# Gate and up projections as seven block products per feature tile instead of eight, and the dense stage in four parts of tiles

## The reference

```python
D_MODEL = 1024
D_FF = 2816

def swiglu(u, w_gate, w_up, w_down):
    return (jax.nn.silu(u @ w_gate) * (u @ w_up)) @ w_down

h = rms_norm(x, g_pre2) * (1 + scale2) + shift2
x = x + gate2 * rms_norm(ffn(h), g_post2)
```

## Time and profile before

| | before |
|---|---|
| median of 3 runs | 2035.15 us |
| the profiled execution, own time | 2034.17 us |
| its span | 2032.4 us |
| granted TensorE clock, mean | 0.976 |
| busy: PE, DVE, ACT, POOL | 1911.1 (94%), 1300.1 (64%), 1084.6 (53%), 96.8 us (5%) |
| gate and up matmuls of the dense stage (L2832) | 2112, first at 472.7, last at 893.9 us |
| down matmuls, parts 1 and 2 (L2864); last part (L2886) | 480, to 809.4 us; 180, to 937.7 us |

### The profile page before, as it was taken

How to read it: one execution, slowest core, us unless ns; L and a number is a source line. 1 busy time by engine, 2 the same in 40 slices (tenths; PEclk the granted TensorE clock), 3 DMA queues, 4 the chain that set the end, 5 groups by cost and what they waited for, 6 DMA issues and landing times. The chain is left out here.

```text
span 2032.4 us, 31748 instructions
## 1 busy us (share of the span) xinstructions
PE 1911.1 (94%) x11144; PEld 1613.2 (79%) x11144; DVE 1300.1 (64%) x1977; ACT 1084.6 (53%) x1781; POOL 96.8 (5%) x64
## 2 busy tenths in 40 slices
PE   5998899899999999998998899889999999999998
PEld 2995575599998998997995665887888888888885
DVE  3735666575223233346817766657888888888888
ACT  4225654454211211236226654547888888888885
POOL 0330000000000000000410000002000000000002
PEclk9998899899999999998999999899999999999999
DMA  6203622202222213212216701149978191918394
GB/s 261 98 27 144 227 85 90 101 18 73 78 83 89 78 52 99 75 61 68 98 47 237 272 23 43 63 154 383 410 283 329 53 360 44 359 63 319 113 320 188
DMA packets 132849, 303.41 MB, mean 149 GB/s; under 512 B 20496, under 2 KB 66448, under 8 KB 129680
## 3 DMA queue, kind: packets, MB, share of 16 engines
q1 hardware_dynamic: 126608, 279.51, 37.9%
q10 hardware_dynamic: 3264, 12.07, 1.5%
q0 software_dynamic: 2880, 10.49, 1.3%
HBM read 360.43 MB, written 28.10 MB: 191 GB/s over the span
## 5 line engine op out<-in xcount | busy, mean ns | idle before, releaser
L2587 DVE TENSOR_TENSOR ex_wl<-ex_raw,ex_wh 128x1024 fp32r<-128x1024 f32 x351 | 419.6, 1223 | 25.8 <-ACT ex_wh L2426 13.8
L2426 ACT ACTIVATE ex_wh<-ex_raw 128x1024 fp32r<-128x1024 f32 x351 | 367.6, 1060 | 70.8 <-PE psum L2506 44.6
L2832 PE MATMUL psum<-norm_out,ex_w_hi 128*128 128x320 f32 x1408 | 268.9, 309 | 2.9 <-PEq L1771 2.9
L2506 PE MATMUL psum<-ex_wh,ex_he_hi 128*128 128x512 f32 (+1 forms) x624 | 242.3, 388 | 4.2 <-DVE ex_wl L2587 3.2
L2506 PE MATMUL psum<-ex_wl,ex_he_hi 128*128 128x512 f32 (+1 forms) x624 | 233.1, 374 | 0.0
L2506 PE MATMUL psum<-ex_wh,ex_he_lo 128*128 128x512 f32 (+1 forms) x624 | 232.6, 373 | 0.0
L2832 PEld LDWEIGHTS psum<-norm_out,ex_w_hi 128*128 128x128 f32 x1408 | 223.1, 188 | 3.2 <-DVE ex_w_lo L2693 3.1
L2693 DVE TENSOR_TENSOR ex_w_lo<-side,ex_w_hi 128x1024 fp32r<-128x1024 f32 (+1 forms) x82 | 82.7, 1015 | 165.4 <-ACT ex_w_hi L2689 165.1
L2832 PE MATMUL psum<-norm_out,ex_w_lo 128*128 128x320 f32 x704 | 165.8, 308 | 0.0
L2767 ACT ACTIVATE ex_sg_hf<-psum 128x640 f32<-128x640 f32 x22 | 15.5, 706 | 235.3 <-PE psum L2832 235.3
L2506 PEld LDWEIGHTS psum<-ex_wh,ex_he_hi 128*128 128x128 f32 x624 | 118.0, 189 | 26.8 <-issue 5.4
(11 more groups left out here) (462 smaller groups left out, 3901.1 us busy)
## 6 DMA issues: line engine op xcount, KB each, us to landing
ex_raw<-moe_gate_up SPq DMA_DIRECT2D x221, 512.0 KB
ex_raw<-moe_w_down SPq DMA_DIRECT2D x143, 512.0 KB
x<-moe_gate_up SPq DMA_DIRECT2D x64, 512.0 KB
wmod_ssd<-w_mod SPq DMA_DIRECT2D x56, 512.0 KB, 5.8
wmod_at<-w_mod SPq DMA_DIRECT2D x24, 512.0 KB, 4.1
side<-ffn_w_gate SPq DMA_DIRECT2D x22, 512.0 KB, 3.9
side<-ffn_w_up SPq DMA_DIRECT2D x22, 512.0 KB, 3.9
mx_qkv_room<-w_in SPq DMA_DIRECT2D x10, 1024.0 KB, 4.9
```

Source lines behind the costliest of these rows:

```text
L2426: act.activation(wh[:, i % RING], raw_of(i), ACT.Copy).then_inc(*hi_done.up(1))
L2506: last = pe.matmul(p.psum[:, 2 + g % 2, 0:width], h[:, k], w[:, i % RING, cols], start=(k == 0 and m == 0), stop=(k == KD - 1 and m == 2))
L2587: dve.tensor_tensor(wl[:, i % RING], raw_of(i), wh[:, i % RING].bitcast(F32), ALU.subtract).then_inc(*lo_done.up(1))
L2832: last = pe.matmul(p.psum[:, home[i] + half, 0:HT], m[:, i % w.RING, cols], x[:, k, half * HT:(half + 1) * HT], start=(k == 0 and n == 0), ...
```

## The change

From the fourth feature tile on, gate and up of a tile are computed together as one product of 2x2 blocks. The tokens are cut in two halves (first, second; 320 each) and the channels in two (top, bottom; 4 blocks of 128 each), which gives token blocks a11, a12 (first half; top, bottom), a21, a22 (second half). The weights have the blocks gate top, gate bottom, up top, up bottom, each 128 x 512 floats. Instead of eight block products there are seven of 12 matmuls each, on combinations:

- tokens: s1 = a21 + a22, s2 = s1 - a11, s4 = a12 - s2, s3 = a11 - a21; made once, on GpSimd (s1, s2, s4: seven additions of 128 x 1280 floats) and VectorE (s3: three), then split in high (ScalarE) and low (VectorE);
- weights, per tile, on VectorE, in the raw room, four subtractions of 512 columns: t1 = up top - gate top, t2 = up bottom - t1, t3 = up bottom - up top, t4 = gate bottom - t2;
- the seven products (`PRODUCTS`) are gate top by a11, t1 by s1, t2 by s2, gate bottom by a12, t3 by s3, up bottom by s4, t4 by a22. t2, t3 and t4 are added in the bank of gate top, up bottom in the bank of t1, and between them the intermediate sums are copied out (ScalarE: `keep_p1`, `keep_p5`, `keep_u2`, 320 columns each) and mixed (VectorE: `mix_gate`, `mix_second`, `mix_first`).

The pieces become entries of 512 columns in rings of 8, made six entries ahead (`ahead_by`). There are four raw rooms. The high part of the hidden tile moves from VectorE to ScalarE (`hidden_high`). The parts are (6, 6, 6, 4). The gate rows are loaded only after the last feature tile, since their room is s1's.

```diff
-DENSE_PARTS = (8, 8, 6)
+DENSE_PARTS = (6, 6, 6, 4)
+PLAIN_F = 3
+PRODUCTS = ("gate_top", "t1", "t2", "gate_bottom", "t3", "up_bottom", "t4")
...
-    RING = 6
+    RING = 8
+    RAW = 4
...
+        @block.gpsimd
+        def _(pool):
+            link = chained(pool_c)
+            pool.wait_ge(*before.low.at(1))
...
+            link(pool, pool.tensor_tensor(s1, plain(a21[0]), plain(a22[0]), ALU.add))
+            link(pool, pool.tensor_tensor(s1, s1, plain(a21[1]), ALU.add))
+            pool.tensor_tensor(s1, s1, plain(a22[1]), ALU.add).then_inc(*token_sum.up())
...
         @block.scalar
...
+            for e in range(n_plain, whole[0]):
+                kind, f, n = entries[e]
+                if kind == "t1":
+                    keep_p1(f)
+                if kind == "t2":
+                    keep_p5(f)
+                if kind == "gate_bottom":
+                    keep_u2(f)
+                if e and entries[e - 1][0] == "t4":
+                    silu_second(entries[e - 1][1])
+                make(e + ahead_by)
+                if kind == "t3":
+                    silu_first(f)
+                if e and entries[e - 1][0] == "t4":
+                    hidden_high(entries[e - 1][1])
...
+            hidden_high(n_f - 1)
+            act.wait_ge(*rows_out.at(16))
+            act.dma_start(rows[:], p.gate_rows.rearrange("q c -> (q c)").partition_broadcast(P)).then_inc(*rows_in.up(16))
...
         @block.tensor
+                if kind == "t1" and f == PLAIN_F:
+                    pe.wait_ge(*token_low.at(3))
+                if kind == "t2":
+                    pe.wait_ge(*copied.at(3 * g + 1))
+                if kind == "t3":
+                    pe.wait_ge(*copied.at(3 * g + 3))
...
+                if kind == "up_bottom":
+                    pe.wait_ge(*copied.at(3 * g + 2))
+                if kind == "t4":
+                    pe.wait_ge(*mixed.at(3 * g + 2))
+                product(e, kind in ("gate_top", "t1", "gate_bottom"))
...
         @block.vector
+            def make(e):
...
+                dve.wait_ge(w.hi_done, e + 1)
+                w.block_low(dve, e)
+                if kind == "gate_top":
+                    dve.wait_ge(*w.arrival(entry_of("up_bottom", f)))
+                    dve.wait_ge(w.lo_done, e + 1)
+                    combine(f, "t1")
...
+            for e in range(n_plain, whole[0]):
+                if kind == "t3":
+                    mix_gate(f)
+                if kind == "up_bottom":
+                    mix_second(f)
+                if kind == "t4":
+                    mix_first(f)
+                make(e + ahead_by)
+                if before_kind == "t4":
+                    multiply(before_f)
+                if e >= 2 and entries[e - 2][0] == "t4":
+                    hidden_low(entries[e - 2][1])
```

More of the change, by code:

```diff
@@ L2835, in features, with product @@
                 return last
+            def product(e, fresh):
+                name, f, _ = entries[e]
+                x_hi, x_lo = moving[name]
+                for k in range(HALF_K):
+                    cols = slice(k * P, (k + 1) * P)
+                    for n, (m, x) in enumerate(((w.wh, x_hi), (w.wh, x_lo), (w.wl, x_hi))):
+                        last = pe.matmul(bank(name, f), m[:, e % w.RING, cols], x[:, k],
+                                         start=(fresh and k == 0 and n == 0), stop=(k == HALF_K - 1 and n == 2),
+                                         skip_group_check=not fresh)
+                last.then_inc(*used.up())
             for i in range(front):
-                pe.wait_ge(w.lo_done, i + 1)
+                pe.wait_ge(w.lo_done, 2 * i + 2)
                 if i == 2:
@@ L2859, in _ @@
                     for b in range(TB):
[L2860 removed]
+                        out = units[part_of[f], n][b]
                         if f == first_of[f]:
[L2862 to L2865 removed]
+                            claim([out])
@@ L2866, in _ @@
+                        for m, (y, x) in enumerate(((hh, w.wh), (hh, w.wl), (hl, w.wh))):
+                            last = pe.matmul(p.psum[:, out, :], y[:, tile, b * P:(b + 1) * P], x[:, e % w.RING, 0:512],
+                                             start=(f == first_of[f] and m == 0), stop=(f == last_of[f] and m == 2))
                         if f == last_of[f]:
                             sums += 1
-                            held[bank] = (evicted, sums)
-                else:
-                    claim([home[i], home[i] + 1])
-                    last = features(i, range(2))
-                    held[home[i]] = held[home[i] + 1] = (taken, f + 1)
@@ L2945, in _ @@
             before.keep_low(dve, TB - 1)
[L2946 to L2958 removed]
+            plain = lambda half: half.bitcast(F32)
@@ L2959, in _ @@
+            for e in range(whole[0] + ahead_by, len(entries)):
+                make(e)
+            multiply(n_f - 1)
+            hidden_low(n_f - 1)
             dve.wait_ge(*rows_in.at(16))
@@ L3079, in build @@
                 p.retire(name)
[L3080 removed]
+            dense = DenseWeights(p, 0, side, above)
             mixer.run(h, None, dense)
```

414 lines of the change are left out of this document (309 added, 105 removed).

## The result

| | before | after |
|---|---|---|
| median of 4 runs, us | 2035.8 | 2054.8 |
| lowest to highest | 2034.5 to 2038.7 | 2051.8 to 2056.7 |
| ratio | | 1.009 (95%: 1.0071 to 1.0108) |
| profiled execution, us | 2034.2 | 2053.2 |
| its span | 2032.4 | 2051.3 |

The change makes the kernel 19 us slower. The forecast was +9.5 us for the profiled execution (+19.0 measured) and 2044 for the median: the direction was right, the size about half. One table shows where the profiled time went. "Stage" runs from VectorE's last low part of the tokens to TensorE's last eight transposes.

What follows compares the result with a forecast made beforehand. TensorE was taken to bound the dense stage. Tiles -12.3, start +9.1 and end +12.7 summed to +9.5 us, taking the profiled 2034.17 to 2043.7; the median was put at 2044, range 2025 to 2055.

Steps and rivals of the forecast that it cites:

- Start: Tile 3: GpSimd additions and VectorE operations hold each other in turns, delaying piece 5 and t2; loss 9.1 us.
- that bound: Start: if multiplies out of PSUM were held by GpSimd too, piece 4 would wait up to 2.9 us more.
- Tiles: The 18 tiles besides tile 3: fewer matmuls, but most of the saving turns into waits; gain 12.3 us.
- through the order rows: Middle tile followed operation by operation across the engines' queues: 13.86 us, not 12.32.
- the walk: Middle tile timed from the end of the t4 before: waits of 0.32 before t2 and 1.22 before t4.
- Rival (c): Dearer hand-overs: 0.5 us more on 14 tiles and 4 more at the start, 2055; chance 0.2.
- Rival (a): The savings land: all 18 tiles take 12.4 to 12.6 us, 2028, or 2020 with mild start; chance 0.2.
- nobody can run ahead: Argument against tiles of 12.4 to 12.6 us: high parts wait for combinations made one step before.
- Down products: Down products in halves, in the dense stage: said to keep their work, forecast 0 us.
- End: Stage's end: late gate rows, late squares, lower clock and VectorE's 7.75 us per block; loss 12.7 us.
- Without the clock and the late squares: Stage's end: last sum 38.5 us behind the last feature product instead of 43.1; loss 8.1 us.
- Behind the stage: Experts behind the dense stage: said to keep their work, forecast 0 us.

Runs made afterwards that it cites:

- e6_fewadds: Changed kernel with three GpSimd additions in place of seven, everything else the same; 1.0035 of the kernel before.
- e9_vector: Changed kernel with its seven GpSimd additions moved to VectorE, same arithmetic; 1.004 of the kernel before.
- e5_p1: Changed kernel with VectorE's mix_second directly behind mix_gate and ScalarE's keep_p1 ahead of hidden_high; 0.9961 of the kernel before.
- e4_parts: Kernel before the change with parts of 6, 6, 6 and 4 tiles and nothing else; 1.0039 of the kernel before.
- e3_ends: Changed kernel with gate rows' DMA issued earlier, Sqrt table load ahead of its wait, row copy behind block 0's squares; 1.0063 of the kernel before.
- e14_rows_again: Changed kernel with only the gate rows' DMA issued early, behind keep_p5 of the last tile; second execution, 1.008 of the kernel before.
- e12_queue: Changed kernel with only ScalarE's table load ahead of the rows' wait and row copy behind block 0's squares; one run, stage 473.9 us.

## Why the prediction was right in direction and half in size

**Start: right in its sum.** +9.1 against +8.8. The turns between GpSimd and VectorE came as walked: a wait of 3.1 (forecast 3.7) before piece 5, then VectorE's backlog. The wait before t2 of tile 3 was 2.1 where 3 to 4 were forecast; two more of 1.5 and 1.6 stand behind it. Of the 8.8 us, e6_fewadds takes 7.5 back with fewer GpSimd additions, and e9_vector 7.0 with none. The rule weighed there, on interfaces that GpSimd shares with VectorE (the Trainium skill, "GPSIMD Engine Reference", section 1, Specifications), agrees with the trace in its named case: the multiply with one input in PSUM took 0.83. So piece 4 was not late, and that bound was rightly left out.

**Tiles: the failed step.** The forecast put a middle tile at 13.86 "through the order rows". The two waits were named rightly: before t2 (0.35 beyond one matmul's distance from start to start, forecast 0.32) and before t4 (1.33, forecast 1.22). What was mis-sized is the hand-overs in the walk. With 0 at the end of the t4 before (635.70), `keep_p1` ends at 3.70, forecast 3.69, and the low part of the next gate top starts at 4.25, forecast 4.26: up to there the walk fits. Then come two rows of VectorE, and the combination for t2 with the high part that ScalarE makes of it:

```profile
639.95 0.69 DVE L2769 TENSOR_TENSOR ex_w_lo<-side,ex_w_hi 128x512 fp32r<-128x512 f32 x1 [1.65 <-ACT ex_w_hi L2766]
640.75 0.69 DVE L3157 TENSOR_TENSOR side<-ex_raw_above,side 128x512 f32<-128x512 f32 x1
...
642.95 0.69 DVE L3157 TENSOR_TENSOR side<-ex_raw_above,side 128x512 f32<-128x512 f32 x1
643.75 0.63 ACT L2766 ACTIVATE ex_w_hi<-side 128x512 fp32r<-128x512 f32 x1 [1.24 <-DVE side L3157]
```

From the combination to the high part, 0.11 us pass here, and 0.11 to 0.12 in all 33 such places at which ScalarE stood waiting for it. The walk took 0.04, the row of a high part and its low part; that hand-over is 0.03 in all 88 places here. The hand-over comes twice ahead of `mix_gate`, for t1 and for t2. Between the low part of gate top and the combination for t1, both on VectorE, pass 0.10 instead of 0.04. That makes 0.21: `mix_gate` starts at 9.93, forecast 9.72, and `mix_second` ends at 12.14, forecast 11.95. It is not the direction that costs: from `mix_gate` to the first SiLU and from the multiply to `hidden_high`, also VectorE to ScalarE, the trace has 0.03 in all 37 places. The difference that it shows is who takes the signal. At the three dear places a semaphore instruction of its own (L2914 on ScalarE, 0.04 us long, L3169 on VectorE, 0.02 us) waits for it ahead of the operation, which itself waits for another one, the weights' arrival; at the cheap places the operation itself waits for it. No run changes this, so that it is the cause is likely, not shown. A second part: the first matmul behind a wait takes 0.22 instead of 0.147 to the next start, 0.08 at t4. Together +0.27 on 11 tiles, +0.38 on three first and +0.1 on four last tiles: with a stall of 0.3 in tile 20, 4.8 us. So the term of the tiles was -12.3 and measured -7.5, half of the 9.4 us by which the forecast was off. Rival (c), dearer hand-overs, named this mechanism; it had 0.5 on 14 tiles and 4 more at the start. Its 2055 is the measured time, but by other terms: some half of its hand-overs, none of its start, and 1.7 + 2.7 us that it did not have. That the stated range up to 2055 still holds the measured 2054.8 is luck to that extent. Rival (a), tiles at 12.4 to 12.6, did not happen, but e5_p1, with tiles of 12.48, shows that only two places in two queues kept it away: "nobody can run ahead" was wrong as a reason. The high parts do wait for combinations; TensorE, however, waited for a sum that could be made 1.3 us earlier.

**Down products: missed.** They were taken to "keep their work". They do, but 540 matmuls of 512 columns stand 0.230 apart, where 480 stood 0.2268 apart before: 1.7 us. The cut into parts of six is not the reason: e4_parts has it, and 180 of its matmuls take 40.85 us (558.35 to 599.20), 0.227 apart as before. What else changed for them is where their operands lie; no run tests that, so the cause stays open.

**End: right by its sum.** +12.7 against +13.2, the five sums within 1.3 us each. It has these parts now: the split alone 5.4 (e4_parts), late rows through ScalarE's queue 3.8 (e3_ends, with the clock lowered as before) and the clock 2.8 (e14_rows_again: 6.6 for both). The remaining 1.2 stand for the most part already at the first sum, 6.8 in e14_rows_again and 5.8 in e4_parts; in the profile after, TensorE waits 0.7 us there for the low part of the last hidden tile, which the forecast had. "Without the clock and the late squares" the forecast had 38.5; e14_rows_again gives 37.0.

**Behind the stage: not in the sum.** 3.1 us of the 18.9 between the spans of the two profiles lie in stages that the change does not touch. A range that takes two single profiles of this kernel has to carry some 3 us for it.

## What to carry to other kernels

When a product is saved on the bounding engine, follow the queue of the engine that feeds it and ask at each wait what stands *ahead* of the awaited instruction; here moving one small addition ahead of work for the next tile won 18.8 us in the stage, about as much as the whole change had lost. Be wary of moving work to GpSimd beside a VectorE that handles SBUF to SBUF: here each instruction of either waited for the end of one of the other's, and the work was cheaper on VectorE itself. Shift a DMA that is wanted at a stage's end to the first point where its room is free, before tuning what waits for it.

## What the runs showed of the hardware that was not expected

- A cast with a single SBUF input is held by GpSimd's additions as well, 3.06 us instead of 0.49; the walk had taken it so, without a row that shows it. (The Trainium skill, "SBUF — State Buffer", section "SBUF: two separate sides", has it so: an fp32 copy from SBUF to SBUF on VectorE uses both ports, and whoever starts first keeps the shared pair for its whole instruction. The trace agrees: the cast, begun at 503.07, ended 0.35 us behind the end of the addition that had begun at 502.80.) Two engines that hold each other in turn lose on both sides: GpSimd's additions took 3.87 to 4.14 us while VectorE had two-input work, 2.98 where it was at the multiply out of PSUM.
- A GpSimd addition of 320 columns takes 0.88 us where nothing holds it, one of 1280 columns 2.98, each with 0.08 behind it: cutting one in four costs 0.8 us.
- Between VectorE and ScalarE 0.03 us pass, in either direction, where the operation itself waits for the signal (125 places in the stage), and 0.11 to 0.12 where a semaphore instruction of its own ahead of it does (33 places).
- Kernels with nearly the same wait of TensorE (2.34 to 2.38 us) and the same matmuls ahead of it had the clock lowered in three profiles and not in three others, each time by the order of ScalarE's work. In e12_queue, behind a wait of 3.5 us, the eight transposes themselves took 1.06 us, as at the full clock, and the mean over the 9 us from their start was yet 0.81.
